# Expert weights in 1 MB units with 19 early places, tokens gathered per pair of experts, and the combine in one run over four banks

## The reference

```
def expert_block(args):
    xb, e = args
    gu = xb @ w_gate_up[e] + b_gate_up[e]
    gate, up = gu[:, :D_EXPERT], gu[:, D_EXPERT:]
    gate = jnp.minimum(gate, SWIGLU_LIMIT)
    up = jnp.clip(up, -SWIGLU_LIMIT, SWIGLU_LIMIT)
    act = (up + 1.0) * (gate * jax.nn.sigmoid(SWIGLU_ALPHA * gate))
    return act @ w_down[e] + b_down[e]
yr = lax.map(expert_block, (xr, block_e)).reshape(n_rows, D)
y = jnp.zeros((T, D), jnp.float32).at[row_tok].add(yr.astype(jnp.float32) * row_g[:, None])
```

## Time and profile before

| what | value |
|---|---|
| three runs | 1418.11, 1415.43, 1417.91 us, median 1417.91 |
| span of the profiled execution | 1413.4 us; its own whole time is not listed, and the median of the runs lies 4.5 us above its span |
| PE busy | 1387.6 us, 98% |
| DVE, ACT, POOL busy | 29%, 18%, 3% |
| read from HBM | 476.6 MB |
| DMA in the expert stage (700 to 1300 us) | 428 GB/s, share 1.01 |
| chain that ended last | PE 88%, DMA 7%, ACT 2%, DVE 2% |

### The profile page before, as it was taken

The page is one execution under the profiler, slowest core; times in us unless marked ns, Lnnn a source line. Parts: engine busy times, 40 slices in busy tenths (PEclk is TensorE's granted clock), DMA queues, the critical chain, the costliest instruction groups (busy, mean ns, idle before and its releaser), DMA issues.

```text
span 1413.4 us, 16428 instructions
## 1 busy us (share of the span) xinstructions
PE 1387.6 (98%) x6520; PEld 735.0 (52%) x6520; DVE 412.3 (29%) x1076; ACT 254.7 (18%) x561; POOL 35.8 (3%) x56
## 2 busy tenths in 40 slices
PE   9999999999999999999999999999999999999897
PEld 8888878888887443343333333334333333343233
DVE  3754465794322121121120211212112021121112
ACT  2113364384102210110100101001010010110002
POOL 1000012110000000000000000000000000000000
PEclk9999999999999999999999999999999999999999
DMA  9444548897975589999999999999999999999994
GB/s 244 148 148 124 175 136 241 277 363 225 299 242 218 211 332 429 428 427 428 428 429 427 428 427 427 428 428 429 427 428 427 427 428 428 428 428 428 426 426 182
DMA packets 105329, 488.63 MB, mean 346 GB/s; under 512 B 10051, under 2 KB 73755, under 8 KB 78583
## 3 DMA queue, kind: packets, MB, share of 16 engines
q1 hardware_dynamic: 96616, 460.47, 81.3%
q0 software_dynamic: 4608, 24.41, 4.9%
q10 hardware_dynamic: 4034, 2.72, 0.7%
HBM read 476.64 MB, written 11.19 MB: 345 GB/s over the span
## 4 chain that ended last, share of the span: by engine, by line
PE 88%; DMA 7%; ACT 2%; DVE 2%; issue 1%; ACTq 0%; POOL 0%; SPq 0%; POOLq 0%; DVEq 0%
PE bank L295 85%; PE bank L891 3%; DMA ring<-in_w_down 2%; DMA ring<-in_w_gate_up 2%; DMA plain_conv<-in_w_down 2%; ACT ring L684 0%; ACT plain_conv L609 0%; DVE ring L1515 0%; ACT ring L640 0%; DVE exn L1515 0%; ACT ring L635 0%; ACT ring L644 0%; ACT ring L633 0%; DVE plain_conv L1512 0%; DVE ring L1512 0%
## 5 line engine op out<-in xcount | busy, mean ns | idle before, releaser
L295 PE MATMUL bank<-ring,plain_conv 128*64 128x512 f32 x2304 | 520.6, 601 | 3.8 <-DMA ring<-in_w_down 3.1
L295 PEld LDWEIGHTS bank<-ring,plain_conv 128*64 128x64 f32 x2304 | 158.5, 138 | 324.3 <-issue 322.1
L295 PE MATMUL bank<-plain_conv 128*64 128x512 f32 (+5 forms) x1072 | 268.6, 526 | 4.8 <-issue 4.4
L295 PE MATMUL bank<-exn,ring 128*128 128x264 f32 (+1 forms) x1168 | 263.9, 387 | 2.8 <-ACT plain_conv L581 2.6
L295 PEld LDWEIGHTS bank<-exn,ring 128*128 128x128 f32 (+1 forms) x1168 | 219.3, 189 | 44.0 <-issue 5.0
L1729 DVE TENSOR_TENSOR xT<-xT,bank 128x264 f32<-128x264 f32 x128 | 55.0, 429 | 489.9 <-PE bank L295 488.9
L295 PEld LDWEIGHTS bank<-plain_conv 128*64 128x64 f32 (+3 forms) x1072 | 115.4, 159 | 100.5 <-issue 95.3
L295 PE MATMUL bank<-exn,plain_conv 128*64 128x512 f32 x384 | 114.7, 596 | 0.1
L787 ACT ACTIVATE plain_conv<-plain_conv 128x512 f32<-128x512 f32 x32 | 20.1, 629 | 381.9 <-DVE plain_conv L1734 381.9
L1734 DVE TENSOR_SCALAR plain_conv<-bank 128x512 f32<-128x512 f32 x32 | 22.0, 688 | 209.7 <-PE bank L295 209.7
L295 PE MATMUL bank<-ring 128*128 128x264 f32 (+3 forms) x520 | 80.4, 336 | 0.0
(11 more groups left out here) (275 smaller groups left out, 650.6 us busy)
## 6 DMA issues: line engine op xcount, KB each, us to landing
ring<-in_w_gate_up SPq DMA_DIRECT2D x96, 2048.0 KB, 22.6
ring<-in_w_down SPq DMA_DIRECT2D x48, 2048.0 KB, 24.8
ring<-in_w_in SPq DMA_DIRECT2D x36, 1024.0 KB, 5.4
exn<-in_w_gate_up SPq DMA_DIRECT2D x15, 2048.0 KB, 23.7
plain_conv<-in_w_gate_up SPq DMA_DIRECT2D x15, 2048.0 KB, 25.4
exn<-in_w_down SPq DMA_DIRECT2D x7, 2048.0 KB, 24.6
plain_conv<-in_w_down SPq DMA_DIRECT2D x7, 2048.0 KB, 24.9
ring<-in_w_proj_b SPq DMA_DIRECT2D x8, 1024.0 KB, 6.8
```

The costliest lines, as they stand in the source:

```text
L295: return nc.tensor.matmul(out, w, x, start=start, stop=stop)
```

## The change

- Weights come in units of 1 MB (`unit_of`): one unit is 128 rows of `w_gate_up` or 256 rows of `w_down`, so one run of memory per partition is 8 KB where it was 16 KB. There are 16 places that go round, and three places (`once`) that are filled once, ahead of everything, and then serve as scratch: 19 MB are placed before the first expert is worked, where it was 16. The early loads stand at other points of SP's queue.
- SP waits for the unit 16 before, in steps of 1 MB. `down(m)` works two units and then counts both.
- `gather` takes a pair's tokens, not a quad's: 24 products of 128 columns per pair with contiguous features, where it was 12 of 256. In the first pair 12 of them precede the first weights and 12 stand behind `gate_up(0, 1)`. The left four groups of features are taken by DVE in one operation (`take_left`), the right four by ACT (`take_right`).
- `combine` runs all its eight products at once, over four banks, behind `gate_up(0, 3)` (in the first pair behind `gate_up(0, 6)`); both turns stand together behind `gate_up(1, 3)`.
- ACT waits for the last tile of `w_out` (`acc_ready` 96, where it was 80) before it issues the load of `b_down`, since `y_out` has moved. Three memsets of DVE move behind `take_left`.
- The last four units of the last pair are columns of `w_down` (`load_columns`), two loads of 0.5 MB each.

```diff
-WIDE = 2 * SLOT
-MSLOT = 8
+ONCE = 3
+MSLOT = 16
...
-CHUNKS = 12
+UNITS = 24
...
-        wide = [ring[:, s * WIDE:(s + 1) * WIDE] for s in range(6)]
-        wide += [exn_t[:, 0:WIDE], pc_t[:, NPLAIN * NT - SLOT:NPLAIN * NT + SLOT]]
+        once = [plain_t[:, SLOT * n:SLOT * n + SLOT] for n in range(ONCE)]
+        unit = [stream[s] for s in (4, 5, 6, 7, 11)]
+        unit += [exn_t[:, 0:SLOT], conv_t[:, 0:SLOT]]
+        unit += [stream[s] for s in (8, 9, 10)]
+        unit += [exn_t[:, SLOT:2 * SLOT], plain_t[:, GB * NT:GB * NT + SLOT]]
+        unit += [stream[s] for s in range(4)]
...
+            def unit_of(j, c):
+
+                if c < 2 * KT:
+                    return w_gu[2 * j + c // KT, P * (c % KT):P * (c % KT) + P, :]
+                x, m = c % 2, (c - 2 * KT) // 2
+                return w_dn[2 * j + x, 2 * P * m:2 * P * m + 2 * P, :].rearrange("(p s) n -> p (s n)", s=2)
...
+            def load_columns(j, c, n):
+
+                h, x = (c - UNITS + 4) // 2, c % 2
+                src = w_dn[2 * j + x, 4 * P:8 * P, 512 * h:512 * h + 512].rearrange("(m p s) n -> m p s n", m=2, s=2)
+                dst = unit[n % MSLOT].rearrange("p (m s n) -> p m s n", m=2, s=2)
+                for m in range(2):
+                    sp.dma_start(dst[:, m], src[m]).then_inc(w_landed[n % MSLOT], 16)
...
+                        sp.wait_ge(S["ysum_ready"], GROUPS + 1)
+                        for n in range(ONCE):
+                            load_once(n)
...
+                    if k == 2 * KT and c >= 5:
+                        load_first(ONCE + 2 * (c - 5), ONCE + 2 * (c - 5) + 2)
+                    if k == KT and w is a["w_out"] and c == 0:
+                        load_first(ONCE + 6, ONCE + 7)
...
+            load_first(ONCE + 7, ONCE + 10)
...
+            load_first(ONCE + 10, ONCE + 12)
+            for s in range(4):
+                sp.wait_ge(S["acc_ready"], free_at[s])
+                load_first(ONCE + 12 + s, ONCE + 13 + s)
...
+                for c in range(first, UNITS):
+                    sp.wait_ge(S["w_used"], PAIRS * UNITS * p + UNITS * j + (c + 1 - MSLOT))
+                    load = load_columns if final and c >= UNITS - 4 else load_unit
+                    load(j, c, UNITS * r + c - ONCE)
...
+            act.wait_ge(S["acc_ready"], 96)
             act.dma_start(y_out[0:E, :], a["b_down"][0]).then_inc(S["bias_loaded"], 16)
+
             def square_u(t, h):
...
+            def take_right(i, u, bank):
+
+                act.wait_ge(S["xt_filled"], 2 * i + 2)
+                for k in range(4, KT):
+                    ins = nc.scalar.activation(xt[u][:, k, :], bank[:, P * (k - 4):P * (k - 4) + P], ACT.Copy, scale=n_ffn[:, k:k + 1])
+                ins.then_inc(S["xt_right"], 1)
...
+            def gather(bank, ks, ts=range(3)):
+
+                for t in ts:
+                    for k in ks:
+                        ins = mm(bank[:, P * (k % 4):P * (k % 4) + P], u_tok[0:ROWS[t], t, P * k:P * k + P],
+                                 pick[0:ROWS[t], t].rearrange("p w s -> p (w s)"), t == 0 and k % 4 == 0, t == 2 and k % 4 == 3)
+                if ts[-1] == 2 and ks[-1] % 4 == 3:
                     ins.then_inc(S["xt_filled"], 1)
...
-                pe.wait_ge(S["comb_emptied"], KT * i + c + 1)
-                mm(p_comb[c % 2][:, 0:NT], y_out[:, P * c:P * c + P], pgt, True, True).then_inc(S["comb_filled"], 1)
+                if c == 0 or c >= 4:
+                    pe.wait_ge(S["comb_emptied"], KT * i + (c - 1 if c else 2))
+                mm(p_comb[c % 4][:, 0:NT], y_out[:, P * c:P * c + P], pgt, True, True).then_inc(S["comb_filled"], 1)
...
+                pe.wait_ge(S["xt_left"], i + 1)
                 if not first:
-                    pe.wait_ge(S["xt_ready"], filled_by_now)
+                    pe.wait_ge(S["xt_right"], i + 1)
                 bias(0)
...
+                for k in range(KT):
+                    if first and k == 4:
+                        pe.wait_ge(S["xt_right"], i + 1)
+                    gate_up(0, k)
+                    if first and k == 1:
+                        gather(p_first[1], RIGHT)
...
+            def take_left(i, u, bank):
+
+                dve.wait_ge(S["xt_filled"], 2 * i + 1)
+                done("xt_left", V.tensor_tensor(xt[u][:, 0:4, :], bank[:, :].rearrange("p (k s) -> p k s", k=4),
+                                                n_ffn[:, 0:4].unsqueeze(2).to_broadcast([P, 4, PAIR]), ALU.mult))
...
+            take_left(0, 0, p_first[0])
+            V.memset(y_out[E:2 * E, :], 0.0)
+            done("comb_emptied", V.memset(y_out[SLOTS:P, :], 0.0))
+            done("comb_emptied", V.memset(pgt, 0.0))
```

More of the change, by code:

```diff
@@ L50 @@
 NSLOT = 12
-WIDE = 2 * SLOT
-MSLOT = 8
+ONCE = 3
+MSLOT = 16
 ROUND = 2
-QUADS = E // 4
-QUAD = 4 * SLOTS
 PAIR = 2 * SLOTS
 PAIRS = E // 2
-CHUNKS = 12
+UNITS = 24
+COLUMN_SLOTS = [(ROUND * UNITS - 4 + n - ONCE) % MSLOT for n in range(4)]
 WARM = 14
@@ L281, in build @@
         landed = [sem(f"stream_landed{i}") for i in range(4)]
+        w_landed = [sem(f"w_landed{i}") for i in range(MSLOT - 4)] + landed
+        before_units = [0] * (MSLOT - 4) + [len(W_COL) + 4] * 4
         dve_step, pool_step = sem("dve_step"), sem("pool_step")
@@ L792, in take_hidden @@
                 nc.scalar.copy(ht[:, w].rearrange("p c s -> p (c s)"), p_ht[:, :]).then_inc(S["ht_ready"], 1)
-            def take_gathered(g, u, b):
-                take_xt(g, u, b, [p_xt[b % 2]] * 2)
-            act.wait_ge(S["nffx_loaded"], 16)
-            for b in range(2):
-                take_xt(0, 0, b, p_first[b], True)
+            take_right(0, 0, p_first[1])
             act.wait_ge(S["gates_in"], 3)
@@ L1235, in down, with gate_up @@
-                def down(kk):
-                    w = [arrived(KT + 2 * kk + x) for x in range(2)]
-                    for c in range(4):
+                def gate_up(x, k):
+                    c = KT * x + k
+                    w = arrived_once(c) if first and c < ONCE else arrived(c)
+                    for n in range(4):
+                        ins = mm(p_gu[x][n // 2][SLOTS * (n % 2):SLOTS * (n % 2) + SLOTS, :],
+                                 xt[r][:, k, SLOTS * x:SLOTS * x + SLOTS], w[:, 512 * n:512 * n + 512], False, k == KT - 1)
+                    ins.then_inc(S["w_used"], 1)
@@ L1238, in down, with down_part @@
+                def down_part(x, m, s, h, w):
+                    return mm(p_y[h][SLOTS * x:SLOTS * x + SLOTS, :], ht[:, x, 2 * (m % 2) + s, SLOTS * (m // 2):SLOTS * (m // 2) + SLOTS],
+                              w, m == s == 0, m == 3 and s == 1)
+                def down(m):
+                    w = [arrived(2 * KT + 2 * m + x) for x in range(2)]
+                    for s in range(2):
                         for h in range(2):
                             for x in range(2):
-                                ins = down_part(w[x], x, kk, c, h)
@@ L1336, in _ @@
+                down_last(0)
+                down_last(1)
+                pe.wait_ge(S["y_half_copied"], p + 1)
+                for t in range(3):
+                    add_last(t, 0)
+                pe.wait_ge(S["y_copied"], i + 2)
+                for t in (2, 0, 1):
+                    add_last(t, 1)
             with pe.Fori(0, n_passes) as p:
                 with pe.If(p > 0):
-                    pe.wait_ge(S["pick_ready"], QUADS * p)
+                    pe.wait_ge(S["pick_ready"], PAIRS * p)
@@ L1339, in _ @@
                     pe.wait_ge(S["y_copied"], PAIRS * p + 1)
-                    for c in range(4):
-                        for t in range(3):
-                            first_part(c, t)
-                pair(p, 0, 0, 0, first=True)
-                pair(p, 0, 0, 1)
-                with pe.Fori(0, QUADS // 2 - 1) as q:
-                    for u in range(2):
-                        for r in range(ROUND):
-                            pair(p, 2 * q + 1 + u, 1 - u, r)
+                    gather(p_first[0], LEFT)
@@ L1349, in _ @@
+                pair(p, 0, 0, first=True)
+                pair(p, 0, 1)
+                with pe.Fori(0, (PAIRS - 4) // 4) as q:
+                    for n in range(4):
+                        pair(p, 2 * q + 1 + n // 2, n % 2)
                 for r in range(ROUND):
-                    pair(p, QUADS - 1, 1, r, True)
+                    pair(p, PAIRS // 2 - 1, r, True)
         @block.vector
```

383 lines of the change are left out of this document (145 added, 238 removed).

## The result

The kernel became slower, by a little. The median is 1421.5 us against 1417.4 for the runs of before beside it; the ratio is 1.0037 (95% interval 1.0019 to 1.0055). Measured once more beside other runs of before (`a_same`), it was 1.0023 (1.0012 to 1.0035), the medians 1421.8 and 1417.5. The loss is 3 to 5 us. Runs at a low granted clock are left out of every ratio, here one of nine (2050.44 us at a mean clock of 0.644) and further down four of the six of `b_16k_1mb`, while one of 1435.9 us (0.946) is kept. The time lies in the range of the prediction and close to its second rival (1422.6), but on the other side of zero than its forecast of 1414.9.

The account below looks back on a forecast made before the run. The weights' DMA stream was taken as the bound, with PE 1% apart. Restart -7.7, rate +5.6 and end -0.9 summed to -3.0 us, from 1417.9 to 1414.9 us; range 1407.5 to 1424.5.

Parts of the forecast that it names:

- second rival: Every transfer from the restart on: 8 KB packets cost their full 13.3 us against 8.6 won; 1422.6 us, chance 0.22.
- What bounds the kernel: Weights' transfers set the end: a pair takes 58.8 us at 428 GB/s, PE 58.3 us on average.
- The sign against it: A DMA share under 0.99 anywhere behind 525 us would mean the stream is no longer the bound.
- Restart of the stream: After the DMA gap at 520 to 525 us, the first `down` frees places earlier: -7.7 us, ends -10 and -3.
- ACT's next square: Before the first gathering, ACT's squares wait for the last tile of `w_out`: +1.7 us for the next one, at 450.50.
- the finer freeing: At the first `down`, two units are counted after eight products, not two chunks after 16: -3.5 us.
- three added places: Filled once ahead of the first expert; seem worth 3 MB or 7.3 us, but claimed not to bring the restart forward.
- Rate of the stream: From the restart on, 8 KB packets instead of 16 KB slow the transfers: +5.6 us, bounds 0 and +13.3.
- The line through 512 B, 1 KB and 16 KB: A packet takes 9.3 ns plus its bytes at 27.2 GB/s, so 8 KB packets give 421.5 GB/s: +13.3 us.
- Behind the last weights: Last pair: a smaller last unit of `w_gate_up` leaves PE less work behind it: -0.9 us, bounds -1.85 and 0.
- The third: At the start, PE idling brings the clock to 1.2 GHz, so the restart gains only 2 us; 1420.6 us, chance 0.10.
- The fourth: PE becomes the bound if the gathering's 24 products take 0.45 us each; about 1428 us, chance 0.06.

Follow-up runs that it names:

- b_16k_1mb: Kernel before with each 2 MB transfer issued as two of 1 MB, for partitions 0 to 63 and 64 to 127, packets still 16 KB; ratio 1.391.
- b_comb: Kernel before with combine's eight products of a pair in one run over four banks, nothing else; 1416.65 us, ratio 0.9988.
- a_comb: Changed kernel with combine's products again two by two between the first expert's units, first pair still in one run; 1422.2 us, ratio 1.0027 to the kernel before.
- b_8k_2mb: Kernel before with 8 KB packets, still 8 places and 2 MB transfers (last pair's column-half loads in two transfers each); 1429.1 us, ratio 1.0081.

## Why the prediction was wrong

**What bounds the kernel** was right: the stream, with PE 1% beside it. `b_comb` and `a_comb` show it from both sides, and the share stayed at 1.01 in the changed kernel. The sign against it, a share under 0.99 somewhere behind 525 us, is in no stretch of 10 us from 530 to 1370.

**Restart of the stream, -7.7 us**, was right in sum (7.8) and mostly in parts. ACT's next square began at 452.43, 1.93 later than 450.50 (forecast +1.7). The first product of `down` came at 512.61 where it had come at 517.00, -4.4 (the terms ahead of the freeing make -4.2). What is left, 3.4, is the finer freeing (-3.5): SP's issue stands 3.68 us behind that product and not 7.11. That the sum is met to a tenth is luck. From the first turn of the router to `down` the changed kernel's two traces take 73.8 and 72.1 us, so one execution is uncertain by more than that. That the three added places are worth nothing there fits, since SP's issue again follows `down` at that fixed distance; no run has them alone.

**Rate of the stream, +5.6 us**, is the step that failed. The line through 512 B, 1 KB and 16 KB said 311 ns a packet and 421.5 GB/s, and the stream ran at 421. It said +13.3. The changed kernel took 13.0 more on the way from the restart to the last unit's products; `b_8k_2mb`, which changes this alone, took 12.6 more there (1388.77 - 524.08 against 852.1) and 11.2 by its medians. My term was +5.6. I had weighed two short stretches with 8 KB packets two to one against that line and called each uncertain by 2%, while the whole question was one of 1.6%. A row whose uncertainty is larger than the effect can't outvote a line through three sizes, each from its own stretch; the one long row in it, 16 KB over 100 us, was the end that counted. The rows of 8 KB had more to say than I read from them, too. Their packets can be timed and not only their bytes, here for 379 to 382 us and for 428 to 432:

```profile
DMA packets 174, 1.29 MB, mean 431 GB/s; under 512 B 16, under 2 KB 16, under 8 KB 16
q1 hardware_dynamic: 174, 1.29, 102.5%
...
q1 hardware_dynamic: 223, 1.70, 101.6%
```

102.5% of 16 x 3 us over 158 long packets is 311 ns, and 101.6% of 16 x 4 us over 206 is 316 ns. Read in the same way, the 16 KB packets from 700 to 800 us (2607 of them, 100.5%) took 617 ns. Two packets of 8 KB are 1.0 to 2.3% dearer than that, so these rows spoke for the line and not against it.

With the line taken whole the same sum gives +4.7, the second rival, and the measured loss is 4.15 and 4.25 by the medians of the two measurements (3.3 and 5.2 by their ratios).

The Trainium skill's rule, "DMA: Bandwidth & Descriptors", section "Why small descriptors are slow (HBM only)", from which I had worked out a loss of 0.8%, fell short as well: 421 to 428 is 1.6%. The measurement decides.

**Behind the last weights, -0.9 us**: 0.6 by the trace, for the reason given, a landing in the way.

**The rivals.** The second one decided "as soon as the stream falls under 423.8 GB/s", and it did; 421 to 422 GB/s was the sign named for it. The third had a mechanism that occurs, a low stretch of the clock (0.57 from 452 to 456 us in the changed kernel), but the restart came all the same, and the products took 0.26 to 0.28. The fourth was ruled out: the gathering's products took 0.28 us, and PE's load fell.

**The chances** were the second error. With 0.22 on a rival for which three rows spoke and against which stood two doubtful ones, the sign of the forecast hung on my choice of a weight.

## What to carry to other kernels

When a change halves the run of memory per partition, price it by the whole stream and by rows long enough to tell the difference; here 8 KB in place of 16 KB cost 13 us on 852, more than a start earlier by 8 us gave. Finer hand-over of places doesn't need finer packets everywhere: only those transfers that end a gap have to be split (that the split is worth its trouble isn't shown). Compare traces by a distance that begins at the event in question; single times ahead of it differ by up to 4 us between executions. And where two resources are within 1% of each other, taking work from one is worth nothing by itself, and pushing its work behind the other's restart brings the pause back a pair later.

## What the runs showed of the hardware

- 16 KB packets to 64 partitions took 1.20 us each on an engine from 700 to 800 us (221 GB/s) and to 128 partitions 0.61 (428 GB/s); the DMA share reads 1.01 in both, so the share doesn't tell a good stream from one at half of its rate. From 1600 to 1700 us the same kernel, with the same share, reached 376 GB/s; why is open.
- 1 MB and 2 MB transfers of the same packets stream alike: 421 GB/s, the DMA share 1.01 in both.
- Two stretches of a lower granted clock far ahead of the work in question (0.91 from 40 to 60 us, 0.85 to 0.89 from 195 to 205) come and go between executions, and move everything behind them by 2 to 4 us. Of the sixteen traces without `b_16k_1mb`'s seven have neither, three the first alone and six both. That these are the three heaps in the run times is likely but not shown.
